# Twelve ring slots, a gather that reads h itself, and expert outputs summed in PSUM

## The chip, the cores and the metric

The kernel runs on one core of a Trainium2 chip. The metric is the device time of one execution in microseconds (us). Everything is float32. One core has a matrix engine (TensorE, PE in the profile; PEld are its loads of the stationary operand), VectorE (DVE), ScalarE (ACT), GpSimd (POOL), and SyncE (SP), which here issues most DMAs. A matmul reads two operands from SBUF, the stationary one (first argument, `[contraction, output rows]`) and the moving one (second argument), and writes one of eight PSUM banks of 128 x 512 float32. A float32 matmul shows as two MATMUL and two LDWEIGHTS records.

## The reference

One encoder block on 256 tokens with 1024 features, then a mixture of experts, then a final norm:

```python
n = rms_norm(h, norm1_g); p = n @ w_in            # q, k, v of two groups of heads
oa = mixer_global(qa, ka, va)                      # 8 heads, all keys, rotary, softmax
ob = mixer_window(qb, kb, vb, sink, rel_bias)      # 8 heads, |i-j| <= 128, bias, sink
h = h + concat[rms_norm(oa, gnorm_a), rms_norm(ob, gnorm_b)] @ w_o
x = rms_norm(h, norm2_g)
gl = x @ w_group + b_group                         # 4 groups, the best one is taken
el = x @ w_expert + b_expert                       # 8 experts a group, the best two are taken
combine[n, e] = softmax weight of the group * normalised weight of the expert
h = h + sum over 32 experts e of
        ((silu(x @ w_gate[e]) * (x @ w_up[e])) * combine[:, e]) @ w_down[e]
out = rms_norm(h, final_g)
```

Each of the 32 experts has three matrices of 1024 x 512 float32, that is 2 MiB each: 96 matrices, 201 MB, all of which are read.

## The kernel before

**Front part.** SP loads the inputs and `w_in`; PE computes q, k, v, the scores, the weighted values and the output projection (`project`) for 8 steps of heads; DVE adds the projections to `h` (128 partitions = tokens, `[t, 1024]` for the two halves t of the tokens). PE begins with three multiplications by a block of zeros (`multiply_zeros`, L1085), which wait for a DVE memset.

**Router.** PE turns `h` (L1093) and multiplies it by the router's weights (`router_logits`, L1249). `ss2`, the sum of squares of each token, comes from ACT (L645, L652); POOL turns it into `rstd2` (L459, L460). DVE computes which two experts each token takes (L879 to L937). Beside it POOL makes `hn = h * norm2_g` (L520), in an order in which each block of 128 features (one `c` of eight, features c, c+8, c+16, ...) lies contiguous, with `norm2_g` broadcast to 128 partitions by a DMA that ACT issues at L642 once the temporary of the attention in the same place (`g2b`) is done with; ACT scales `hn` by `rstd2` (L656).

**Experts.** They are worked on in ten units of 2 or 4 experts (`WAYS = 2,2,4,4,2,2,4,4,4,4`), 128 rows to a unit: 64 or 32 token places for each expert. For unit i:
- DVE makes `pick` (L944), a matrix of zeros and ones: which token goes to which place, and `pick_w` (L952), the same with the expert's weight.
- PE gathers (L1284): `xgT[:, c, :] = hn[:, t, c, :]^T @ pick[:, t, :]`, 8 blocks c times 2 halves t, 32 MATMUL records a unit, into two banks, which ACT (L665) and DVE (L956) copy to `xgT`.
- `products` (L1322, for the first unit `first_gate`, L1383): gate and up, with `xgT` stationary and the weights moving; `silu` (ACT), `product` (DVE); `turn_act` (L1333) transposes the result; `down` and `early_down` (L1339).
- `turn_picks` (L1302) transposes `pick_w`, DVE copies it to `place_w`, and `scatter` (L1373) multiplies it by the unit's output `y_slots`: 4 results of 128 x 512, in two banks used in turn. DVE adds each to `h` (`add_outputs`, L971, 36 additions, and 4 more at the end, L1044), and `sc_free` tells PE that the bank is free.

PE's order in iteration i: first half of the gather of i, `turn_act(i-1)`, second half, `down(i-1)`, gate of i, `scatter(i-2)`, up of i with `turn_picks(i)` in its middle. In `turn_act` the stationary operand is read with a step of four elements:

```python
act_c = act_sb.rearrange("p (k c) -> p c k", c=FC)
last = pe.transpose(ps[TR][:, c * P:(c + 1) * P], act_c[:, c, :], ident)
```

**The ring.** All matrices go through `RING = 11` slots of 16 KB a partition (2 MiB each). The 96 matrices have fixed places in a sequence (`fill_at(unit, gate/up/down, expert)`); number f goes to slot f mod 11, and may be loaded when number f-11 has been used (`wait_used`). The first four experts (units 0 and 1, numbers 0 to 11) are fixed; the other 28 are put in an order that depends on the counts of tokens (`order_ready`, after DVE L1001), and SP reads their numbers with `value_load`. In the front part slots 5 to 10 hold attention data, and SP waits until it is done with before it loads them (L322): number 8 at `projected` 4, number 9 at `weighted_v` 8, number 10 at `projected` 8. Numbers 11 and 12 follow in quarters (L360, L366), as the first gate product uses up slots 0 and 1; the next eleven in halves and quarters (L374); all later ones whole. The last unit's down matrices come in pieces (`LAST_PIECES`).

**The end.** PE multiplies the last pieces (with a multiplication by constants between them, `multiply_constants(1, TR)`, L1268), scatters (L1459), DVE adds to `h`, ACT takes squares (L701), POOL and DVE turn the sums into `rstdf` (L526 to L535, L1075), DVE and ACT scale by `rstdf` and `final_g` (L1078, L706) and the result is stored. `final_g` is broadcast by a DMA at L661.

## Time and profile before

| | |
|---|---|
| median of 3 runs | 571.07 us (570.36 to 571.14) |
| profiled execution | 570.79 us, its span 569.0 us |
| PE, DVE, ACT, POOL busy | 451.1, 116.3, 63.5, 29.1 us |
| mean granted PE clock | 0.902 |
| moved by DMA | 218.72 MB, 384 GB/s over the span |

```profile
span 569.0 us, 6262 instructions
DMA  8989991658999999999999999999999999999992
GB/s 303 382 330 428 424 361 49 285 185 272 384 399 422 429 428 423 428 431 428 423 430 427 427 427 428 428 428 424 430 428 428 426 427 428 428 427 428 418 381 88
PE 49%; DMA 45%; POOL 2%; DVE 1%; issue 1%; SPq 1%; ACT 0%; DVEq 0%; ACTq 0%; POOLq 0%
```

The span is the time from the first to the last instruction; the execution takes 1.8 us more. The second and third line cut the span into 40 slices of 14.2 us: the busy share of the 16 DMA engines in tenths, and what they moved. The last line is the chain of waits that ended last, by engine.

### The profile page before, as it was taken

Reading aid. Unit: us, or ns where it says so; the run is one execution under the profiler, and the core shown is the slowest. Engines: PE = TensorE matmul, PEld = TensorE weight load, DVE = VectorE, ACT = ScalarE, POOL = GpSimd, SP = SyncE. Lnnn points to the kernel's source line nnn. Section 1 sums busy time; section 2 is a strip of 40 time slices with the busy share of each in tenths; the row PEclk is TensorE's granted clock in tenths of the full one; section 3 lists DMA queues with packets and bytes.
Section 4 is the critical chain, followed back from the end, with each engine's and each line's share of the span. In section 5 each row is a group of like instructions: output and inputs, shape, how many; then the busy total and the mean of one; then the engine's idle time right before and its main releaser. Section 6 shows DMA issues by size and latency. Waiting matters only on the chain.

```text
span 569.0 us, 6262 instructions
## 1 busy us (share of the span) xinstructions
PE 451.1 (79%) x2546; PEld 199.9 (35%) x2546; DVE 116.3 (20%) x281; ACT 63.5 (11%) x130; POOL 29.1 (5%) x58
## 2 busy tenths in 40 slices
PE   8999999989999994596999938753855475566874
PEld 3456676564535241141353502230213121311221
DVE  2017764251101210220222202010201002100413
ACT  1125332131000100100101001000000001000103
POOL 0232200220000000000000000000000000000002
PEclk9999999999999996887999978787878767886999
DMA  8989991658999999999999999999999999999992
GB/s 303 382 330 428 424 361 49 285 185 272 384 399 422 429 428 423 428 431 428 423 430 427 427 427 428 428 428 424 430 428 428 426 427 428 428 427 428 418 381 88
DMA packets 27679, 218.72 MB, mean 384 GB/s; under 512 B 5465, under 2 KB 6745, under 8 KB 14849
## 3 DMA queue, kind: packets, MB, share of 16 engines
q1 hardware_dynamic: 23120, 215.09, 91.2%
q10 hardware_dynamic: 4528, 3.22, 1.8%
q8 instruction: 21, 0.34, 0.2%
q14 instruction: 10, 0.07, 0.0%
HBM read 217.23 MB, written 1.06 MB: 384 GB/s over the span
## 4 chain that ended last, share of the span: by engine, by line
PE 49%; DMA 45%; POOL 2%; DVE 1%; issue 1%; SPq 1%; ACT 0%; DVEq 0%; ACTq 0%; POOLq 0%
DMA ring<-in_w_gate_dram 21%; PE bank L1322 19%; DMA ring<-in_w_up_dram 12%; DMA ring<-in_w_down_dram 9%; PE bank L1101 7%; PE bank L1339 6%; PE bank L1284 3%; PE bank L1173 3%; PE bank L1163 2%; DMA g2b<-in_norm_g_dram 2%; PE bank L1373 2%; PE bank L1141 1%; PE bank L1383 1%; PE bank L1152 1%; DMA ring<-in_w_in_dram 1%
## 5 line engine op out<-in xcount | busy, mean ns | idle before, releaser
L1322 PE MATMUL bank<-ring,region_x 128*32 128x512 f32 (+1 forms) x992 | 155.9, 681 | 76.7 <-DMA ring<-in_w_gate_dram 48.8
L1322 PEld LDWEIGHTS bank<-ring,region_x 128*32 128x32 f32 (+1 forms) x992 | 45.0, 129 | 178.8 <-issue 178.8
L1339 PE MATMUL bank<-ring,region_q 128*32 128x512 f32 (+1 forms) x512 | 81.1, 677 | 27.8 <-DMA ring<-in_w_down_dram 25.3
L971 DVE TENSOR_TENSOR h<-h,bank 128x512 f32<-128x512 f32 x36 | 24.7, 687 | 218.0 <-PE bank L1373 218.0
L1339 PEld LDWEIGHTS bank<-ring,region_q 128*32 128x32 f32 (+1 forms) x512 | 23.6, 129 | 77.6 <-issue 72.6
L677 ACT ACTIVATE region_x<-bank 128x512 f32<-128x512 f32 x20 | 11.1, 595 | 286.6 <-PE bank L1373 251.4
L1101 PE MATMUL bank<-ring,region_x 128*128 128x512 f32 x96 | 42.6, 596 | 0.3 <-DMA ring<-in_w_in_dram 0.3
L1284 PEld LDWEIGHTS bank<-region_q,region_t 128*128 128x128 f32 x320 | 37.4, 192 | 8.6 <-issue 8.6
L1284 PE MATMUL bank<-region_q,region_t 128*128 128x128 f32 x320 | 40.1, 278 | 0.3 <-DVE region_q L944 0.3
L1373 PE MATMUL bank<-region_x,region_q 128*128 128x512 f32 x72 | 35.0, 618 | 1.2 <-ACT region_x L677 1.2
L1173 PE MATMUL bank<-ring,region_q 128*128 128x512 f32 x64 | 28.9, 597 | 0.0
L1101 PEld LDWEIGHTS bank<-ring,region_x 128*128 128x128 f32 x96 | 17.8, 190 | 23.2 <-issue 21.6
L526 POOL TENSOR_TENSOR region_t<-h,g2b 128x512 f32<-128x512 f32 x1 | 1.3, 1268 | 442.5 <-ACT region_q L701 442.5
L1373 PEld LDWEIGHTS bank<-region_x,region_q 128*128 128x128 f32 x72 | 11.4, 188 | 24.8 <-DVE h L971 11.8
L665 ACT ACTIVATE region_x<-bank 128x512 f32<-128x512 f32 x10 | 6.0, 597 | 113.8 <-PE bank L1284 113.8
L944 DVE TENSOR_TENSOR region_q<-cst,region_t 128x256 f32<-128x256 f32 x8 | 3.4, 426 | 73.2 <-PE bank L1302 73.2
L1173 PEld LDWEIGHTS bank<-ring,region_q 128*128 128x128 f32 x64 | 11.6, 190 | 12.6 <-issue 12.6
L1163 PE MATMUL bank<-region_v,ring 128*128 128x65 f32 x128 | 15.2, 272 | 0.0
L1163 PEld LDWEIGHTS bank<-region_v,ring 128*128 128x128 f32 x128 | 15.0, 192 | 0.5 <-issue 0.5
L965 DVE TENSOR_TENSOR region_q<-region_q,bank 128x512 f32<-128x512 f32 x10 | 6.9, 688 | 31.1 <-PE bank L1322 31.1
L791 DVE SCALAR_TENSOR_TENSOR h<-bank,stat,h 128x512 f32<-128x512 f32 x8 | 6.0, 751 | 20.6 <-PE bank L1173 17.8
L960 DVE COPY region_q<-bank 128x512 f32<-128x512 f32 x10 | 6.9, 692 | 15.9 <-PE bank L1333 15.9
(192 smaller groups left out, 263.0 us busy)
## 6 DMA issues: line engine op xcount, KB each, us to landing
ring<-in_w_gate_dram SPq DMA_DIRECT2D x28, 2048.0 KB, 32.6
ring<-in_w_up_dram SPq DMA_DIRECT2D x28, 2048.0 KB, 34.0
ring<-in_w_down_dram SPq DMA_DIRECT2D x24, 2048.0 KB, 35.9
ring<-in_w_down_dram SPq DMA_DIRECT2D x10, 1024.0 KB, 13.6
ring<-in_w_up_dram SPq DMA_DIRECT2D x6, 1024.0 KB, 12.2
ring<-in_w_in_dram SPq DMA_DIRECT2D x8, 512.0 KB, 8.5
ring<-in_w_o_dram SPq DMA_DIRECT2D x2, 2048.0 KB, 12.6
ring<-in_w_down_dram SPq DMA_DIRECT2D x8, 512.0 KB, 12.1
```

Source lines behind the costliest of these rows:

```text
L665: act.activation(xgT[:, 0:4, :], ps[GD0][:].rearrange("p (c s) -> p c s", c=4), ACT.Copy).then_inc(xg_act, 1)
L677: act.activation(y_slots[:, 512 * half:512 * half + 512], ps[GD0 + half][:], ACT.Copy).then_inc(y_ready, 1)
L960: dve.tensor_copy(hT, ps[TR][:].rearrange("p (c s) -> p c s", c=FC)).then_inc(hT_ready, 1)
L965: dve.tensor_tensor(act_sb, silu_sb, ps[UP][:], ALU.mult).then_inc(act_done, 1)
L971: dve.tensor_tensor(part, part, ps[SC0 + k % 2][:], ALU.add).then_inc(sc_free, 1)
L1101: return pe.matmul(ps[bank][:], xT[:, c, t * P:(t + 1) * P], cols, start=(c == 0), stop=(c == KC - 1))
L1163: last = pe.matmul(ps[6][:, 65 * l:65 * l + 65], probsT[:, s % 2, kt, l, :], v_sb[:, kt, 2 * g + l // 2, :], start=(kt == 0), stop=(kt == ...
L1173: last = pe.matmul(ps[bank][:], mixT[:, 1 - g, t, c - 4 * g, :], w_o_sb[g][:, c - 4 * g, 512 * half:512 * half + 512], start=(c == 4 * g), ...
L1284: last = pe.matmul(ps[GD0 + b][:, c * P:(c + 1) * P], hn[:, t, 4 * b + c, :], pick[:, t, :], start=(t == 0), stop=(t == TT - 1))
L1322: last = pe.matmul(ps[bank][rows, :], xgT[:, c, rows], slots[fill_slot(f + a)][:, c * F:(c + 1) * F], start=(c == 0), stop=(c == KC - 1))
L1339: last = pe.matmul(ps[GD0 + half][rows, :], hT[:, c, rows], slots[fill_slot(f + a)][:, c * D + 512 * half:c * D + 512 * half + 512], start ...
L1373: last = pe.matmul(ps[SC0 + k % 2][:], place_w[:, (k // 2) * P:(k // 2 + 1) * P], y_slots[:, 512 * (k % 2):512 * (k % 2) + 512], start=Tru ...
```

## The change

- `RING` is 12. The places of `qkT`, `v_sb` and the attention's temporaries, which were tensors of their own (`region_t`, `region_v`, `g2b`), now lie in slot 11 (`late`) and are done with before number 11 is loaded there: SP waits for `sso_ready` 4 (the last sum of squares of the attention's output), between numbers 9 and 10. The refill in pieces now begins with number 12, and both first matrices belong to unit 2, so both need `order_ready`.
- `hn` is gone, with POOL L520, ACT L656 and the broadcast DMA of `norm2_g`. The gather reads `h` itself, as stationary operand with a step of eight elements (`h_cols`). `pick` holds `rstd2` instead of one, and is made by one `tensor_scalar` for each half and expert; so is `pick_w`. `norm2_g` is applied when `xgT` is cut out of PSUM: ACT in four pieces, DVE by a `tensor_tensor`.
- The scatter adds up in four banks (Y0 to Y3) over all units; the 36 additions of DVE and `sc_free` go. `turn_picks` and `turn_act` use the GATE bank: `turn_picks` waits for `silu_done`, `turn_act` for `place_ready`. `place_w` has two buffers.
- At the end DVE adds `h` and the four banks into `h_sum`. `final_g` is spread by matmuls (`spread_final_g`) in place of the multiplications by constants, and copied by ACT; the sum for `rstdf` is one instruction of DVE, only the power is left to POOL.
- At the start PE multiplies 4.5 blocks of zeros from a constant and waits for nothing, where it had multiplied 3 after a memset.

```diff
-RING = 11
+RING = 12
+        late = slots[QKT_SLOT]
+        q_tmp = late[:, 3080:3592].rearrange("p (h d) -> p h d", h=8)
-        hn = region_t[:, 0:2048].rearrange("p (t c k) -> p t c k", t=TT, c=KC)
+        h_cols = h.rearrange("p t (k c) -> p t c k", c=KC)
+        h_sum = slots[TAIL_SLOT][:, 2048:4096].rearrange("p (t d) -> p t d", t=TT)
...
             load(1, 1, 1, 3)
+            sp.wait_ge(sso_ready, 4)
+            load(1, 2, 1, 3)
             sp.wait_ge(projected, 8)
             load(1, 2, 0, 2)
...
+            sp.wait_ge(order_ready, 1)
+            experts = order_of(2, range(1))
+            for c in range(PIECES):
+                if c < PIECES - 1:
+                    sp.wait_ge(gate_pieces, c + 1)
+                else:
+                    sp.wait_ge(gate_done, 1)
+                load_piece(2, 0, 0, c, PIECES)
+                if c == 0:
+                    experts += order_of(2, range(1, 2))
+                if c == 2:
+                    experts += order_of(2, range(2, 4))
+                load_piece(2, 0, 1, c, PIECES)
...
-                pool.tensor_tensor(hn[:, t].rearrange("p c k -> p k c"), h[:, t, :].rearrange("p (k c) -> p k c", c=KC),
-                                   g2b[:].rearrange("p (k c) -> p k c", c=KC), ALU.mult).then_inc(hg_ready, 1)
...
-                act.activation(hn[:, t], hn[:, t], ACT.Copy, scale=rstd2[:, t:t + 1]).then_inc(hn_ready, 1)
...
-                act.activation(xgT[:, 0:4, :], ps[GD0][:].rearrange("p (c s) -> p c s", c=4), ACT.Copy).then_inc(xg_act, 1)
+                for c in range(4):
+                    last = act.activation(xgT[:, c, :], ps[GD0][:, c * P:(c + 1) * P], ACT.Copy, scale=g2_rows[:, c:c + 1])
...
+                for t in range(TT):
+                    for a in range(n_e):
+                        last = dve.tensor_scalar(pick[:, t, rows * a:rows * (a + 1)], iota1[:, 0:rows],
+                                                 ranks[:, t, e0 + a:e0 + a + 1], rstd2[:, t:t + 1], ALU.is_equal, ALU.mult)
...
-                    dve.tensor_tensor(part, part, ps[SC0 + k % 2][:], ALU.add).then_inc(sc_free, 1)
...
-                        last = pe.matmul(ps[GD0 + b][:, c * P:(c + 1) * P], hn[:, t, 4 * b + c, :], pick[:, t, :],
+                        last = pe.matmul(ps[GD0 + b][:, c * P:(c + 1) * P], h_cols[:, t, 4 * b + c, :], pick[:, t, :],
...
-                    pe.wait_ge(place_ready, i)
+                    pe.wait_ge(silu_done, i + 1)
...
-                    pe.wait_ge(sc_free, 4 * i + k + 1)
-                    last = pe.matmul(ps[SC0 + k % 2][:], place_w[:, (k // 2) * P:(k // 2 + 1) * P],
-                                     y_slots[:, 512 * (k % 2):512 * (k % 2) + 512], start=True, stop=True)
+                    last = pe.matmul(ps[Y0 + k][:], place_w[i % 2][:, (k // 2) * P:(k // 2 + 1) * P],
+                                     y_slots[:, 512 * (k % 2):512 * (k % 2) + 512], start=(i == 0), stop=False)
...
-            pe.wait_ge(zeros_ready, 1)
-            multiply_zeros(3)
+            zeros = nc.const_aps.tensor(0.0, (P, 512), F32)
+            for cols in (512, 512, 512, 512, 256):
+                pe.matmul(ps[6][:, 0:cols], zeros[:, 0:P], zeros[:, 0:cols], start=True, stop=True)
...
+            def spread_final_g(half, bank):
+                for k in range(4):
+                    c = 4 * half + k
+                    last = pe.matmul(ps[bank][:, k * P:(k + 1) * P], final_g_cols[:, c:c + 1].broadcast_to([P, P]), ident,
+                                     start=True, stop=True)
+                last.then_inc(final_g_turned, 1)
...
             last_products(0)
+            spread_final_g(0, UP)
             last_products(1)
-            multiply_constants(1, TR)
+            spread_final_g(1, GATE)
             last_products(2)
-            multiply_constants(1, TR)
             last_scatter(0)
             last_products(3)
...
+            dve.wait_ge(ssf_ready, 3)
+            dve.scalar_tensor_tensor(rstdf[:, 0:1], ssf[:, 0:1], EPS, ssf[:, 1:2], ALU.add, ALU.add).then_inc(mean_ready, 1)
```

## Rows read from the trace of the kernel before

**Rows 1.** The span cut into stages: busy time of each engine, PEclk, DMA share, GB/s.

```profile
85.00:95.00 10.00, 10.00 (x53) 6.79 (x53) 4.89 (x13) 3.27 (x8) 0.73 (x2) 1.00 0.01 2
95.00:128.00 33.00, 31.51 (x159) 19.99 (x159) 12.75 (x53) 7.70 (x14) 6.91 (x8) 1.00 0.59 223
128.00:141.00 13.00, 12.87 (x72) 5.75 (x70) 2.81 (x10) 2.47 (x3) 0.00 (x0) 1.00 0.81 258
141.00:153.00 12.00, 11.12 (x70) 6.45 (x66) 2.40 (x4) 0.60 (x1) 0.00 (x0) 1.00 1.02 409
...
210.00:550.00 340.00, 236.49 (x1442) 86.63 (x1434) 43.68 (x72) 14.61 (x27) 0.00 (x0) 0.84 1.01 427
```

**Rows 2.** DMA issues of the page: KB each, median us from issue to landing.

```profile
ring<-in_w_gate_dram SPq DMA_DIRECT2D x28, 2048.0 KB, 32.6
```

**Rows 3.** SP's DMA issues around the router, from the timeline: start, us.

```profile
96.23 2.06 SPq L322 DMA_DIRECT2D ring<-in_w_up_dram  x2
113.07 0.33 SPq L322 DMA_DIRECT2D ring<-in_w_down_dram  x1
128.58 0.33 SPq L360 DMA_DIRECT2D ring<-in_w_down_dram  x1
```

**Rows 4.** The chain of waits from 97 to 127 us: start, us, what.

```profile
99.47 11.92 DMA g2b<-in_norm_g_dram
...
117.42 0.56 POOL stat L460
...
118.00 0.43 DVE region_q L879 x2
...
123.61 2.92 PE bank L1284 x24
```

**Rows 5.** Timeline of the router: the last sum of squares, the last logits.

```profile
114.95 0.20 ACT L652 ACTIVATION_READ_ACCUMULATOR region_q<-h 128x1 f32 x1
...
115.49 2.03 PE L1249 MATMUL bank<-region_t,region_x 128*128 128x36 f32 x16
```

**Rows 6.** PE records by source line: ns min/median/max, first and last start, form.

```profile
L1383 PEld LDWEIGHTS bank<-ring,region_x x32: 132/137/137, 126.6 to 134.8; 128*64 128x64 f32 x32
L1302 PEld LDWEIGHTS bank<-cst,region_q x20: 138/140/143, 131.1 to 540.5; 128*128 128x128 f32 x20
L1333 PEld LDWEIGHTS bank<-cst,region_q x40: 195/209/218, 145.7 to 545.6; 128*128 128x128 f32 x40
L1333 PE MATMUL bank<-cst,region_q x40: 277/283/385, 145.8 to 545.8; 128*128 128x128 f32 x40
L1284 PEld LDWEIGHTS bank<-region_q,region_t x320: 186/192/201, 123.6 to 490.7; 128*128 128x128 f32 x160
```

**Rows 7.** Timeline of PE: runs of matmuls with few moving columns.

```profile
96.04 1.89 PE L1163 MATMUL bank<-region_v,ring 128*128 128x65 f32 x16
...
145.84 0.64 PE L1333 MATMUL bank<-cst,region_q 128*128 128x128 f32 x4
```

**Rows 8.** DVE and ACT operations by source line: ns min/median/max.

```profile
L944 DVE TENSOR_TENSOR region_q<-cst,rank x2: 416/420/425, 123.0 to 132.0; 128x256 f32<-128x256 f32 x2
L725 DVE TENSOR_SCALAR region_x<-region_x,gT x8: 346/350/354, 5.7 to 11.9; 128x256 f32<-128x256 f32 x8
L665 ACT ACTIVATE region_x<-bank x10: 597/597/598, 125.7 to 488.9; 128x512 f32<-128x512 f32 x10
```

**Rows 9.** Timeline of PE's start.

```profile
1.58 5.26 PE L1085 MATMUL bank<-region_t 128*128 128x512 f32 x6 [1.58 <-DVE region_t L720]
...
7.12 5.39 PE L1101 MATMUL bank<-ring,region_x 128*128 128x512 f32 x12 [0.28 <-DMA ring<-in_w_in_dram]
```

**Rows 10.** Timeline of the end: last square, last power, last two outputs.

```profile
562.64 0.19 ACT L701 ACTIVATION_READ_ACCUMULATOR region_q<-h 128x1 f32 x1
...
563.64 0.54 POOL L535 TENSOR_TENSOR stat<-stat 128x1 f32<-128x1 f32 x1
563.71 1.41 DVE L1078 SCALAR_TENSOR_TENSOR region_t<-h,stat,g2b 128x512 f32<-128x512 f32 x2 [0.31 <-POOL stat L533]
```

More of the change, by code:

```diff
@@ L675, in down_out @@
                 for half in range(2):
+                    if i == UNITS - 1:
+                        act.wait_ge(final_g_turned, half + 1)
+                        act.activation(final_gb[:, 512 * half:512 * half + 512], ps[(UP, GATE)[half]][:], ACT.Copy).then_inc(final_g_cut, 1)
                     act.wait_ge(down_done, 2 * i + 1 + half)
@@ L965, in product @@
                 dve.tensor_tensor(act_sb, silu_sb, ps[UP][:], ALU.mult).then_inc(act_done, 1)
-            def add_outputs(i):
-                for k in range(4):
-                    dve.wait_ge(scattered, 4 * i + k + 5)
-                    part = h[:, k // 2, 512 * (k % 2):512 * (k % 2) + 512]
-                    dve.tensor_tensor(part, part, ps[SC0 + k % 2][:], ALU.add).then_inc(sc_free, 1)
             def places_out(i):
                 dve.wait_ge(picks_turned, i + 1)
-                dve.wait_ge(scattered, 4 * i + 4)
-                dve.tensor_copy(place_w, ps[PW][:, 0:256]).then_inc(place_ready, 1)
+                if i > 1:
+                    dve.wait_ge(scattered, 4 * i)
+                dve.tensor_copy(place_w[i % 2], ps[PICKS0 if i == 0 else GATE][:, 0:256]).then_inc(place_ready, 1)
             make_picks(rank1, 0, 2)
-            dve.engine_nop().then_inc(sc_free, 2)
             k_w = mark(dve.tensor_tensor(w2, w1, e2, ALU.mult))
@@ L1042, in _ @@
                 dve.wait_ge(scattered, 4 * UNITS + k + 1)
-                part = h[:, t, 512 * half:512 * half + 512]
-                dve.tensor_tensor(part, part, ps[(SC0, SC1, GATE, UP)[k]][:], ALU.add).then_inc(sc_free, 1)
+                dve.tensor_tensor(h_sum[:, t, 512 * half:512 * half + 512], h[:, t, 512 * half:512 * half + 512],
+                                  ps[Y0 + 2 * t + half][:], ALU.add).then_inc(summed, 1)
             over = dve.value_load(over_flag[0:1, 0:1], min_val=0, max_val=1)
@@ L1048, in _ @@
                 ov_nT_sb = slots[3].rearrange("p (c t) -> p c t", c=16)
+                link(dve.tensor_tensor(weight_over, weight_over, bcast(rstd2, 2, EXPERTS), ALU.mult))
                 for t in range(TT):
@@ L1064, in _ @@
                         for half in range(2):
-                            part = h[:, t, 512 * half:512 * half + 512]
+                            part = h_sum[:, t, 512 * half:512 * half + 512]
                             last = dve.tensor_tensor(part, part, ps[3 + half][:], ALU.add)
@@ L1082, in _ @@
         def _(pe):
-            def multiply_zeros(n):
-                for _ in range(n):
-                    pe.matmul(ps[6][:], zeros[:, 0:P], zeros[:, P:P + 512], start=True, stop=True)
-            pe.wait_ge(zeros_ready, 1)
-            multiply_zeros(3)
+            zeros = nc.const_aps.tensor(0.0, (P, 512), F32)
+            for cols in (512, 512, 512, 512, 256):
+                pe.matmul(ps[6][:, 0:cols], zeros[:, 0:P], zeros[:, 0:cols], start=True, stop=True)
             def turn(dst, srcs, done):
@@ L1331, in turn_act @@
                 pe.wait_ge(act_done, i + 1)
+                pe.wait_ge(place_ready, i + 1)
                 for c in range(FC):
-                    last = pe.transpose(ps[TR][:, c * P:(c + 1) * P], act_c[:, c, :], ident)
+                    last = pe.transpose(ps[GATE][:, c * P:(c + 1) * P], act_c[:, c, :], ident)
                 last.then_inc(act_turned, 1)
@@ L1398, in _ @@
             for k in range(2 * TT):
-                last = pe.transpose(ps[SC0][0:EXPERTS, k * P:(k + 1) * P], (rank1, weight)[k // TT][:, k % TT, :], ident)
+                last = pe.transpose(ps[RANKS][0:EXPERTS, k * P:(k + 1) * P], (rank1, weight)[k // TT][:, k % TT, :], ident)
             last.then_inc(ranks_turned, 1)
@@ L1481, in _ @@
                     else:
-                        pe.wait_ge(sc_free, 4 * UNITS + 2)
+                        pe.wait_ge(summed, 4)
                     for b in range(2):
                         for c in range(4):
-                            last = pe.transpose(ps[5 + b][:, c * P:(c + 1) * P], hn[:, t, 4 * b + c, :], ident)
+                            last = pe.transpose(ps[5 + b][:, c * P:(c + 1) * P], h_cols[:, t, 4 * b + c, :], ident)
                     last.then_inc(ov_turned, 1)
```

244 lines of the change are left out of this document (105 added, 139 removed).

## The prediction, made before the changed kernel ran

> **What bounds the kernel now.** I read the page's busy shares first, then the span cut into stages. From 210 to 550 us the DMA engines are busy all the time (share 1.01) and move 427 GB/s, while PE works 236 of 340 us [rows 1]. There only bytes count. Before that lies the hole that the change can reach: from 85 to 95 us 2 GB/s are moved, from 95 to 128 us 223 GB/s, from 128 to 141 us 258 GB/s [rows 1]. The reason is in SP's issues: nothing is loaded after the transfer issued at 113.07 us until a slot comes free at 128.58 us [rows 3], though 96 - 11 = 85 matrices are still to come. So the time is: the moment T0 at which slot 0 begins to come free, plus the matrices still missing then, plus what idles until the queue is full, plus an end after the last piece.
>
> T0 hangs on a chain: ACT issues the broadcast of `norm2_g` at 99.47 us, it lands 11.92 us later, then POOL makes `hn` and the power (the last ends at 117.98), DVE decides (118.00 on), PE gathers from 123.61 on [rows 4].
>
> **The change part by part.**
>
> *The twelfth slot.* One matrix is 2048 KB = 2.097 MB [rows 2]; at 427 GB/s [rows 1] that is 4.91 us. It counts in full if number 11 is there before T0 and the DMA engines are the bound afterwards. SP issues two matrices from 96.23 us [rows 3]; number 11 comes right behind them, since `sso_ready` 4 falls in the 0.2 us before 99.47 [rows 4], where ACT issued the next thing in its program. Three matrices from 96.2 on take 14.7 us, to 111; number 10, issued at 113.07, takes 4.9, to 118. T0 is ten us later. Its wait has number 10 queued behind it on SP, which waits for something later anyway. After T0 the same bytes come free at the same pace, so the lead of one matrix stays. **-4.9 us.** Its other end is 0, if the lead is lost somewhere. The pieces of refill are as many and as large as before; both now wait for `order_ready`, which comes with DVE L1001, behind the gather's end at 126.53 [rows 4] and some two us before 128.58; the first `value_load` falls into that time. 0.
>
> *The router's chain.* Without broadcast, POOL L520 and ACT L656, `rstd2` needs only the last sum of squares, there at 114.95 + 0.20 = 115.15 [rows 5], and POOL's two small operations (0.56 for the power [rows 4], less for the other): 116.1. Now the logits are late: PE ends them at 115.49 + 2.03 = 117.52 [rows 5]. DVE starts at 117.55 instead of 118.00 [rows 4]: **-0.45** (bounds -0.9 and 0).
>
> *The first picks* are on the chain. One `tensor_tensor` of 256 columns takes 0.42 us; now four `tensor_scalar` of 64. The nearest row is `tensor_scalar` on 256 columns, 0.35 [rows 8]. Four as one, 0.35, is the lower end (-0.07); four at 0.2 one after the other, 0.8, the upper (+0.4). They don't depend on each other and overlap in part: **+0.15**. The eight and eight of a four-way unit lie on DVE beside the second half of the up product, and after 210 us beside 104 us in which PE waits anyhow [rows 1]; uncovered before 210 they might cost 2 us once.
>
> *The gather reads with a step of eight.* This is the unknown. LDWEIGHTS takes 137 ns for 64 columns (L1383) and 192 for 128 (L1284) [rows 6]: 0.86 ns a column and 82 fixed. A transpose with packed columns takes 140 (L1302), 0.45 a column; the same with a step of four elements, 16 bytes, 209 (L1333) [rows 6]: (209 - 82)/128 = 0.99 ns a column. So a step costs a transpose's load 69 ns. What decides is how far apart the pairs come: n of them last n - 1 spacings and one record of 0.28 [rows 6]. Where only 65 columns move, the load sets it: 16 in 1.89 us is 0.107 [rows 7], near 128 x 0.86. The gather's 24 in 2.92 us [rows 4] make 0.115; the four stepped transposes in 0.64 [rows 7] make 0.119. No row has a stepped load that is no transpose. Three answers:
>  (a) the load goes at the slower of its own pace and the stepped one, 0.99 ns a column: spacing 0.127, +0.012 a record;
>  (b) the 69 ns come on top of 0.107: 0.176, +0.061;
>  (c) a plain float32 load needs two stepped passes of 0.127: 0.254, +0.139.
> Of these I take (a): 0.86 and 0.99 lie side by side, and it looks as if the plain load already runs slowly enough to hide most of the step.
> What one record costs the end: 24 lie before T0, 8 before the third quarter of slots 0 and 1 is free, so 32 in full. The 32 of unit 1 lie between the freeing of the up slots and of the down slots. There the queue has just run out: 13 us at 258 and 12 us at 409 GB/s are 8.26 MB moved from 128 to 153 us [rows 1], of the 8.39 MB of the four slots freed; I count 1 us of slack (0 to 2). After that slots come free faster than they are filled, and more delay is hidden. Cost: 32x + max(0, 32x - 1). (a) **+0.4**, (b) 1.95 + 0.95 = 2.9, (c) 4.45 + 3.45 = 7.9 us.
>
> The Trainium skill bears on this: "SBUF — State Buffer", section "Door 1: The DMA port swizzle", says that SBUF is read in lines of 16 bytes and that each step to a new line pays a penalty, so that a step of four float32 is the last free one. By that rule the gather, at 32 bytes, is slowed, as in (b) or (c), and the change loses half its gain or all of it. The trace agrees in so far as L1333 pays 69 ns, and that already at four elements. The same skill, "TensorE: Matmul & The Clock Gate", section "LDWEIGHTS", puts a load at the columns divided by 1.2 in ns; the 0.86 ns a column of the plain load fits that, the 0.45 of a transpose does not.
>
> *xgT* is cut in four pieces by ACT. Whole it took 0.60 us [rows 8]. The first piece can take no longer, and PE has 8 gather records, 0.92 us, in between; the next chunks are further apart. 0. In later units it lies beside the second half of the gather. If it didn't: four times 0.6 less 0.6, 1.8 us, and only before 153 us.
>
> *Scatter, 36 additions gone, new waits.* DVE's 36 additions stood beside PE. `turn_picks` waits for `silu_done`, and silu (one ACT pass) has the scatter and half the up product to be done in; behind it on PE stand the rest of the up product and so the next slots. `turn_act` waits for `place_ready`, which DVE gives before the product that `turn_act` waits for anyway. 0; the bound is one ACT pass, 0.6 [rows 8], in unit 1, which has no scatter ahead. Scatters without `sc_free` can only gain, and PE has time there.
>
> *The start.* Before, six zero records take 5.26 us from 1.58 on, 0.86 each, and the first real ones follow at 7.12, 12 in 5.39 us or 0.43 each [rows 9]: the first go at half the rate, which is that of the lower level of PE's clock (1.2 of 2.4 GHz), though the granted clock is given as 1.00. Nine records of 512 columns now start some 0.65 us earlier, at about 0.95. If they stay slow as long as before, until between 6 and 7.1 us less those 0.65, some three are left to run at 0.43: end between 7.1 and 7.6. If the rate changes at the same moment as before, up to 7.9. If it came at once, they would end long before 7.12, and the data would be late next. From there to the router PE works without a gap, so a late start reaches T0. **+0.25** (0 to +0.75).
>
> *The end.* The last square is there at 562.83, POOL's last power starts only at 563.64, and DVE's two outputs run from 563.71 to 565.12 [rows 10]. Now the sum is one DVE operation (0.2) behind the square, the power (0.54) follows: 562.9 + 0.2 + 0.1 + 0.54 = 563.8 for the second half, whose output of 0.7 ends at 564.5; the first half's is done by then. **-0.6** (-1.0 to 0). `spread_final_g` stands where constants were multiplied.
>
> Sum: -4.9 - 0.45 + 0.15 + 0.4 + 0.25 - 0.6 = **-5.15 us**. The profiled execution took 570.79 (span 569.0 and 1.8 around it): 565.6; the median of the runs is 0.28 higher: **565.9 us**.
>
> **The rivals.**
> 1. *The stepped load costs its 69 ns in full (b).* -5.55 + 2.9 = -2.65: 568.4. For it: L1333; against it: the two paces side by side.
> 2. *Slower: the stepped load needs two slow passes (c).* Place: the gathers of units 0 and 1. -5.55 + 7.9 = +2.35: 573.4. It decides from 64x - 1 = 5.55, a spacing of 0.115 + 0.102 = 0.217 us or more. For it: a plain load costs twice a transpose's packed one a column (0.86 to 0.45), as if it read everything twice.
> 3. *The lead is lost* (number 11 is late or PE is the bound between 153 and 210 us): only the small terms are left, about 570.8. Against it: share 1.01 for 340 us.
> 4. *More is won*: PE, without waits for banks, frees slots sooner between 128 and 160 us, where the queue runs dry: another 2 us, 563.9.
>
> **How the numbers follow.** Forecast 0.54, rival 1 0.20, rival 2 0.11, rival 3 0.07, rival 4 0.08. The forecast's own range is 564.8 to 567.2, from its small terms. To leave out no more than two in ten the range takes in rivals 1 and 4 and ends short of rivals 2 and 3: **563.6 to 570.0**. A change under 0.2% (1.1 us) can't be told from none. Faster: forecast, rivals 1 and 4, less a little for unseen stalls, 0.80; within 0.2%: most of rival 3, 0.08; slower: rival 2 and such stalls, 0.12.
>
> **What would show it.** Number 11 issued near 99.7 us; DMA idle from 118 to about 128; the chain runs through PE's logits, not through a broadcast; L1284's successor at 24 in about 3.2 us and LDWEIGHTS near 209 ns (261 for rival 1, 335 for rival 2); first refill near 128.9; 427 GB/s from 210 us on and the last piece about 4.6 us sooner; the last output ending 1.7 us behind the last square instead of 2.3. It would be wrong if the first refill came later than 130 us or the DMA share fell below 1 after 160 us.

## The result and the profile after

The changed kernel takes **578.88 us** (median of 4 runs, 576.27 to 579.52), the kernel before 571.11 in the same session: ratio 1.0117, 95% interval 1.0085 to 1.0149. It is 7.8 us slower. The profiled execution took 579.32 us, its span is 577.1. So 2.2 us lie outside the span, where the kernel before has 1.8.

The page of the kernel after, its span, DMA share and GB/s (40 slices), and the weight loads of the gather:

```profile
span 577.1 us, 6390 instructions
...
DMA  8979992925979999999999999999999999999981
GB/s 307 379 297 433 420 363 104 363 116 185 372 265 427 405 404 429 433 422 430 425 428 429 426 426 428 426 430 425 430 428 424 432 424 429 430 425 428 421 343 75
...
L1263 PEld LDWEIGHTS bank<-region_q,h 128*128 128x128 f32 x320 | 77.7, 334 | 9.1 <-issue 8.2
```

The same windows as in [rows 1] (length, then busy us and instructions of PE, PEld, DVE, ACT and POOL, granted clock, DMA share, GB/s), kernel after:

```profile
95.00:128.00 33.00, 32.26 (x134) 20.72 (x133) 13.38 (x56) 5.01 (x11) 2.19 (x6) 0.88 0.65 255
128.00:141.00 13.00, 12.87 (x62) 8.08 (x63) 3.27 (x13) 3.01 (x6) 0.00 (x0) 0.92 0.42 141
141.00:153.00 12.00, 12.00 (x59) 6.39 (x55) 2.06 (x8) 0.60 (x1) 0.00 (x0) 1.00 0.90 319
153.00:160.00 7.00, 6.12 (x29) 5.56 (x30) 1.38 (x2) 1.14 (x4) 0.00 (x0) 1.00 0.92 383
160.00:190.00 30.00, 29.12 (x134) 16.03 (x132) 5.74 (x20) 2.93 (x7) 0.00 (x0) 1.00 0.92 357
190.00:210.00 20.00, 20.00 (x132) 6.68 (x132) 0.00 (x0) 1.58 (x3) 0.00 (x0) 1.00 0.99 395
210.00:550.00 340.00, 258.99 (x1508) 120.00 (x1504) 37.68 (x125) 19.01 (x49) 0.00 (x0) 0.89 1.01 427
```

The plateau from 210 us on is what it was, 427 GB/s. More is moved ahead of T0: 255 against 223 GB/s from 95 to 128 us. The 32 GB/s more are 1.06 MB; the kernel before also moved its two broadcasts there, so the twelfth matrix (2.10 MB) is the gain. (Without its early load, but otherwise with the changed front part, it is 191 GB/s, in e9 and e5 below.) But the hole behind it is deeper, 141 against 258 GB/s and 319 against 409 [rows 1], and it lasts: the full rate holds only from 210 us on.

One instruction has become slower, the weight load of the gather (count, then minimum, median and maximum in ns, start of the first and last):

```profile
L1263 PEld LDWEIGHTS bank<-region_q,h x320: 312/335/340, 125.6 to 501.5; 128*128 128x128 f32 x160
```

Before, it took 192 ns [rows 6]. From the chain of waits of the kernel after (start, duration, engine, what, line, records):

```profile
117.67 5.89 PE bank L1247 x8
...
124.52 0.99 DVE region_q L934 x4
...
125.56 6.00 PE bank L1263 x24
...
150.08 4.00 PE bank L1263 x16
...
180.56 4.00 PE bank L1263 x16
...
214.94 4.00 PE bank L1263 x16
...
237.81 39.02 DMA ring<-in_w_gate_dram
```

The first 24 records take 6.00 us where they took 2.92 [rows 4]: their spacing is (6.00 - 0.28)/23 = 0.249 us. It is the same in the 16 of unit 1, (4.00 - 0.28)/15 = 0.248, at a granted clock of 1.00, so the lower clock in part of the first gather (0.92 from 128 to 141 us) is not the reason. And the chain stays on PE, through the gathers of units 1, 2 and 3, until it goes over to a DMA at 237.81.

SP's issues of the kernel after; the second row is the first refill, which was at 128.58 [rows 3]:

```profile
99.06 13.94 SPq L324 DMA_DIRECT2D ring<-in_w_down_dram  x2
...
133.77 17.91 SPq L361 DMA_DIRECT2D ring<-in_w_gate_dram  x12
```

The prediction had named two signs that it would be wrong: a first refill later than 130 us, and a DMA share below 1 after 160 us. Both are there, 133.77 and 0.92.

### The profile page after: what moved, and what is told of

It is laid out like the page before. It is cut to its first block, busy times and chain, and to the rows that moved or that the text cites. A ratio compares the mean times of both kernels' runs of the same rounds, so it can differ in the third digit from the quotient of the medians.

```text
span 577.1 us, 6390 instructions
## 1 busy us (share of the span) xinstructions
PE 482.0 (84%) x2562; PEld 244.6 (42%) x2562; DVE 110.0 (19%) x353; ACT 67.9 (12%) x160; POOL 23.6 (4%) x53
## 3 DMA queue, kind: packets, MB, share of 16 engines
HBM read 216.19 MB, written 1.06 MB: 376 GB/s over the span
## 4 chain that ended last, share of the span: by engine, by line
PE 55%; DMA 41%; DVE 1%; SPq 1%; issue 1%; DVEq 0%; POOL 0%; ACT 0%
DMA ring<-in_w_up_dram 33%; PE bank L1301 18%; PE bank L1080 7%; PE bank L1263 7%; DMA ring<-in_w_gate_dram 7%; PE bank L1319 6%; PE bank L1152 5%; PE bank L1142 2%; PE bank L1120 1%; PE bank L1352 1%; PE bank L1365 1%; PE bank L1072 1%; PE bank L1131 1%; PE bank L1247 1%; DMA ring<-in_w_in_dram 1%; SPq L324 1%
## 5 line engine op out<-in xcount | busy, mean ns | idle before, releaser
L1263 PEld LDWEIGHTS bank<-region_q,h 128*128 128x128 f32 x320 | 77.7, 334 | 9.1 <-issue 8.2
L1263 PE MATMUL bank<-region_q,h 128*128 128x128 f32 x320 | 80.5, 407 | 0.7 <-DVE region_q L934 0.7
L1319 PE MATMUL bank<-ring,region_q 128*32 128x512 f32 (+1 forms) x512 | 73.1, 609 | 9.3 <-DMA ring<-in_w_down_dram 6.7
L667 ACT ACTIVATE region_x<-bank 128x512 f32<-128x512 f32 x20 | 11.1, 595 | 237.8 <-PE bank L1352 222.3
L648 ACT ACTIVATE region_x<-bank,gT 128x128 f32<-128x128 f32 x40 | 11.4, 367 | 139.9 <-PE bank L1263 139.9
L520 POOL TENSOR_TENSOR ring<-ring 128x512 f32<-128x512 f32 x1 | 1.3, 1275 | 452.8 <-ACT region_q L691 452.8
L1142 PEld LDWEIGHTS bank<-ring 128*128 128x128 f32 x128 | 15.0, 192 | 0.5 <-issue 0.5
L1142 PE MATMUL bank<-ring 128*128 128x65 f32 x128 | 15.2, 272 | 0.0
L950 DVE TENSOR_TENSOR region_x<-bank,gT 128x512 f32<-128x512 f32 x10 | 6.9, 692 | 33.5 <-PE bank L1263 33.5
L943 DVE TENSOR_SCALAR region_q<-cst,sorted_rw 128x32 f32<-128x32 f32 (+1 forms) x56 | 12.4, 301 | 0.0
L934 DVE TENSOR_SCALAR region_q<-cst,sorted_rw,stat 128x32 f32<-128x32 f32 (+1 forms) x56 | 12.4, 299 | 0.0
```

The source lines that it names most:

```text
L648: last = act.activation(xgT[:, c, :], ps[GD0][:, c * P:(c + 1) * P], ACT.Copy, scale=g2_rows[:, c:c + 1])
L667: act.activation(y_slots[:, 512 * half:512 * half + 512], ps[GD0 + half][:], ACT.Copy).then_inc(y_ready, 1)
L934: last = dve.tensor_scalar(pick[:, t, rows * a:rows * (a + 1)], iota1[:, 0:rows], ranks[:, t, e0 + a:e0 + a + 1], rstd2[:, t:t + 1], ALU.i ...
L943: last = dve.tensor_scalar(pick_w[:, t, rows * a:rows * (a + 1)], iota1[:, 0:rows], ranks[:, t, e0 + a:e0 + a + 1], weights[:, t, e0 + a:e ...
L950: dve.tensor_tensor(xgT[:, 4:8, :], ps[GD1][:].rearrange("p (c s) -> p c s", c=4), bcast(g2_rows[:, 4:8], 2, P), ALU.mult).then_inc(xg_dve, 1)
L1142: last = pe.matmul(ps[6][:, 65 * l:65 * l + 65], probsT[:, s % 2, kt, l, :], v_sb[:, kt, 2 * g + l // 2, :], start=(kt == 0), stop=(kt == ...
```

## The experiments

Fifteen experiments ran, one of them (e12) the changed kernel again. Times are medians; a ratio is to the kernel before in the same session (571.14 to 571.63 us), with its 95% interval.

### The step by itself, taken away and put in

**e2_after_packed**, the kernel after, with the gather reading 128 columns that lie together. This leaves out the order of the features, so the experts compute something else, with the same work; the same holds for e3, e5, e8 to e11 and e15:

```diff
-last = pe.matmul(..., h_cols[:, t, 4 * b + c, :], pick[:, t, :],
+last = pe.matmul(..., h[:, t, (4 * b + c) * P:(4 * b + c + 1) * P], pick[:, t, :],
```

> The changed kernel, but the gather reads h in packed blocks of 128 columns. This leaves out the order of the features (the experts get wrong rows of the weights), the work is the same. Theory 1: 8.0 us (between 7.6 and 8.6) less than the changed kernel, that is 570.3 to 571.3 us, first refill issued near 129.5 us instead of 133.8. Theory 2: no more than 3 us less, over 575.9 us.

Measured: 567.49 us, 0.9929 (0.9905 to 0.9952). That is lower than either expectation had it. The step alone costs 578.88 - 567.49 = **11.4 us** by the medians and 10.7 by the two ratios, with some 2 us of uncertainty either way. Windows and chain of e2:

```profile
128.00:141.00 13.00, 12.87 (x72) 5.75 (x72) 4.35 (x18) 2.66 (x4) 0.00 (x0) 1.00 0.67 219
141.00:153.00 12.00, 11.12 (x70) 6.45 (x68) 2.07 (x3) 1.14 (x4) 0.00 (x0) 1.00 0.99 383
153.00:160.00 7.00, 7.00 (x35) 2.77 (x33) 0.00 (x0) 1.19 (x2) 0.00 (x0) 1.00 1.00 360
160.00:190.00 30.00, 29.12 (x180) 12.81 (x180) 5.74 (x20) 1.74 (x5) 0.00 (x0) 1.00 1.02 422
190.00:210.00 20.00, 20.00 (x158) 8.97 (x154) 5.74 (x20) 2.71 (x7) 0.00 (x0) 1.00 1.02 429
```

```profile
117.52 0.43 DVE region_q L868 x2
...
123.60 4.31 PE bank L1263 x24
...
203.66 33.91 DMA ring<-in_w_up_dram
```

Against the rows of after, the five windows from 128 to 210 us lack (219 - 141) x 13 + (383 - 319) x 12 + (360 - 383) x 7 + (422 - 357) x 30 + (429 - 395) x 20 kB = 4.25 MB; at 427 GB/s that is 10.0 us, of the 11.0 between the two profiled executions (579.32 and 568.30). More than half of it, 2.63 MB, is missing after 160 us, where I had counted on cover. Here the chain leaves PE at 203 us, not at 237.

**e1_before_stepped**, the kernel before with `hn` laid out in `h`'s order, so that its gather steps by eight. POOL's multiplication and ACT's scaling then go through `hn` in the other order, but take what they took (2.35 and 1.14 us, before 2.37 and 1.15):

```diff
-hn = region_t[:, 0:2048].rearrange("p (t c k) -> p t c k", t=TT, c=KC)
+hn = region_t[:, 0:2048].rearrange("p (t k c) -> p t c k", t=TT, c=KC)
...
-act.activation(hn[:, t], hn[:, t], ...)
+act.activation(hn[:, t].rearrange("p c k -> p k c"), hn[:, t].rearrange("p c k -> p k c"), ...)
```

> The kernel before, with one edit: hn is stored in the order of h, so that the gather reads it with a step of eight elements, as the changed kernel does. Theory 1 (a plain float32 load makes two slow passes when its columns are stepped): records 0.249 us apart instead of 0.115, 24 x 0.134 = 3.2 us before the first gate product, 8 x 0.134 = 1.1 before the third quarter of slots is free, 32 x 0.134 - 1 = 3.3 in unit 1: 7.6 us slower, 578.7 us, LDWEIGHTS 335 ns. Theory 2 (the stepped load is mostly hidden by the DMA queue, and the loss comes from the clock drop at 116 us, the picks and the end): at most 2 us slower, under 573.1 us.

Measured: 580.89 us, 1.0158 (1.012 to 1.0195), +9.6 us. The weight load of e1:

```profile
L1284 PEld LDWEIGHTS bank<-region_q,region_t x320: 312/335/338, 123.7 to 504.2; 128*128 128x128 f32 x160
```

So the cost belongs to the stepped operand, not to the ring, the PSUM banks or the new picks. It is the price that rival 2 put on it; that the load really makes two passes, no run shows.

### How large a step

**e8_steps_by_unit** gives each of the ten units a step of its own; one execution.

```diff
+steps_of = (8, 8, 1, 2, 4, 8, 1, 2, 4, 8)
+def block_of(t, c):
+    s = steps_of[unit_now[0]]
+    return h[:, t].rearrange("p (b k s) -> p b s k", k=P, s=s)[:, c // s, c % s, :]
```

> The changed kernel with another step in each unit's gather: 8, 8, 1, 2, 4, 8, 1, 2, 4, 8 elements (features come in the wrong order where it isn't 8). Theory X (SBUF is read in lines of 16 bytes, each new line costs): packed 192 ns for a LDWEIGHTS, step 2 in between or as packed, steps 4 and 8 alike, 335 ns. Theory Y (the cost grows with the step): step 4 clearly below step 8, near 260 ns, as the transposes with step 4 (209 ns, 69 more than packed) would say if the 69 ns were simply added.

Its weight loads in the gathers of units 1, 2, 3 and 8, steps 8, 1, 2 and 4 in this order:

```profile
L1270 PEld LDWEIGHTS bank<-region_q,h x32: 312/335/336, 147.9 to 155.7; 128*128 128x128 f32 x32
...
L1270 PEld LDWEIGHTS bank<-region_q,h x32: 186/192/202, 178.4 to 182.3; 128*128 128x128 f32 x32
...
L1270 PEld LDWEIGHTS bank<-region_q,h x32: 192/196/208, 208.8 to 212.9; 128*128 128x128 f32 x32
...
L1270 PEld LDWEIGHTS bank<-region_q,h x32: 308/329/329, 430.5 to 438.2; 128*128 128x128 f32 x32
```

Steps of 1, 2, 4 and 8 take 192, 196, 329 and 335 ns: a cliff between 8 and 16 bytes, and nearly flat on both sides of it. The execution took 573.47 us, near the kernel in which units 0 and 1 step and the others are packed (574.42, next).

### Where the step costs time

The same edit in some units only, on the base of e2: in units 0 and 1 (**e10_stepped_early**), in 2 to 9 (**e11_stepped_late**), in 0 to 2 (**e15_stepped_012**); and the kernel after once more beside the first two (**e12_after_again**).

```diff
-if unit_now[0] < 2:      # e10; e11 swaps the two results
+if unit_now[0] < 3:      # e15
     return h_cols[:, t, c, :]
 return h[:, t, c * P:(c + 1) * P]
```

> The changed kernel, with the step of eight only in the gathers of units 0 and 1, and packed blocks (wrong order of features) in units 2 to 9. By the place named in the prediction (only units 0 and 1 reach the end) the whole loss stays: 578.9 us. If unit 2, which also comes before the queue is full for good, matters as well: 1 to 3 us less, 576 to 578 us.

> The reverse: packed in units 0 and 1, the step of eight in units 2 to 9, which costs PE 4 us a unit. By the prediction the DMA queue hides all of it: 567.5 us, as the packed kernel. If not, up to 3 us more, and the DMA share falls below 1 somewhere after 180 us.

> The changed kernel once more, beside the others on the same chip: 578.9 us. Its trace tells whether the fall of the granted clock stands at 116 to 123 us again. If it is a property of the kernel's program it comes at the same place; if it wanders, it comes elsewhere between 112 and 130 us, and the mean over runs holds a part of it.

> The step of eight in units 0, 1 and 2, packed blocks (wrong order of features) in units 3 to 9. Stepped in units 0 and 1 only it was 574.4 us, in all units 578.8. If unit 2 is the rest: 577 to 578.8 us. If it is not (the rest is the clock's fall, which hits only some programs): 574.4 to 575.5 us.

| stepped in | us | ratio (95%) |
|---|---|---|
| none (e2) | 567.49 | 0.9929 (0.9905 to 0.9952) |
| units 2 to 9 (e11) | 568.87 | 0.9953 (0.9932 to 0.9974) |
| units 0 and 1 (e10) | 574.42 | 1.0063 (1.0033 to 1.0093) |
| units 0 to 2 (e15) | 578.13 | 1.0126 (1.0108 to 1.0144) |
| all (e12) | 578.75 | 1.0115 (1.0095 to 1.0136) |

By the medians units 0 and 1 cost 6.9 us and unit 2 another 3.7; both are clear of the intervals, which leave each some 2 us of room. The 0.6 of units 3 to 9 and the 1.4 of units 2 to 9 alone (e11) are inside them. The two parts alone, 6.9 and 1.4, fall short of the 11.4 of all: by the medians, a late gather hurts when the queue is behind already. I had expected 576 to 578.9 for e10. The windows of e10, then those of e15:

```profile
160.00:190.00 30.00, 29.13 (x152) 13.55 (x150) 5.74 (x20) 2.93 (x7) 0.00 (x0) 1.00 0.99 386
190.00:210.00 20.00, 20.00 (x152) 6.68 (x149) 4.36 (x18) 1.58 (x3) 0.00 (x0) 1.00 1.02 427
```

```profile
160.00:190.00 30.00, 29.13 (x134) 16.03 (x132) 5.74 (x20) 2.93 (x7) 0.00 (x0) 1.00 0.97 379
190.00:210.00 20.00, 20.00 (x136) 6.44 (x136) 0.36 (x2) 1.57 (x3) 0.00 (x0) 1.00 1.00 400
```

In e10 the rate is back at 427 from 190 us on; with unit 2 stepped too it is at 400 until 210. From 128 to 210 us e15 moves 0.75 MB less than e10, or 1.8 us; the two profiled executions lie 2.8 us apart (576.62 and 573.79). e10 and e12 ran in one session, e2 and e15 in others, so differences across them carry the sessions' own, up to half a microsecond.

### The slot, its lead, and its capacity

**e9_packed_eleven_used** is e2 with the loads in the order and at the distance of the kernel before: twelve slots are there, eleven fills are ahead. **e5_packed_no_lead** is e2 with number 11 issued behind the first refill's wait instead of early.

```diff
 load(1, 1, 1, 3)                 # both
-sp.wait_ge(sso_ready, 4)
-load(1, 2, 1, 3)
...
+if c == 0:                       # e5; e9: waits on FILLED_BY[f - 11]
+    load(1, 2, 1, 3)
```

> The packed kernel with twelve slots, but SP's program and PE's waits for pieces of the kernel before: number f is loaded when number f - 11 has been used, so that only eleven slots are ever full. Theory of capacity (until 153 to 160 us the queue runs dry, so that then all free slots are filled, and what counts is how many slots there are, not when the twelfth was filled): 4.9 us more than the packed kernel, 572.4 us. Rival (the twelfth slot gave nothing, as holding back its first load cost only 0.7 us; what the packed kernel gained came from the router and the missing broadcasts): 567.5 to 568.5 us.

> The packed kernel of the second experiment (the gather takes packed blocks, so features come in the wrong order), with the load of number 11 held back until the first quarter of slot 0 comes free: twelve slots, but only eleven filled when the refill begins. If the twelfth slot is worth its lead (one matrix at 427 GB/s), this is 4.9 us slower than the packed kernel: 572.4 us. If the lead is lost later anyway, no change: 567.5 us.

e9: 572.24 us, 1.0009 (0.9996 to 1.0023), so the slot is worth 572.24 - 567.49 = **4.75 us**, or 4.4 if each is taken against the kernel before in its own session (+0.6 and -3.8). e5: 568.2 us, 0.9934 (0.9914 to 0.9954), only 0.7 us above e2, inside the intervals. The windows of e5:

```profile
128.00:141.00 13.00, 12.87 (x76) 6.36 (x76) 4.98 (x23) 3.61 (x7) 0.00 (x0) 1.00 0.68 242
141.00:153.00 12.00, 11.12 (x69) 6.30 (x67) 2.17 (x4) 1.14 (x4) 0.00 (x0) 1.00 1.03 423
153.00:160.00 7.00, 7.00 (x36) 2.88 (x34) 0.00 (x0) 1.19 (x2) 0.00 (x0) 1.00 1.00 412
```

The queue of e2 runs dry from 128 to 160 us (219, 383, 360 GB/s) and e5 moves more in those gaps (242, 423, 412). That is 1.14 MB, a good half of the late matrix. The reading that fits both runs is that what counts is how many slots are there for the queue until PE is ahead of it, not how early the twelfth is filled.

### The small terms

**e3_packed_tt_picks**: e2 with the picks in one `tensor_tensor`, `rstd2` left out. **e4_after_short_start**: the kernel after with three zero blocks in place of five. **e14_after_one_constant**: the kernel after with a fourth of the constants' products ahead of the ranks.

```diff
-for a in range(n_e):                          # e3, for each t
-    last = dve.tensor_scalar(pick[...], iota1[:, 0:rows], ranks[...], rstd2[:, t:t + 1], ALU.is_equal, ALU.mult)
+dve.tensor_tensor(to, bcast(...iota1[:, 0:rows]...), bcast(ranks[...], 3, rows), ALU.is_equal)
-for cols in (512, 512, 512, 512, 256):        # e4
+for cols in (512, 512, 512):
-multiply_constants(4, GATE)                   # e14
+multiply_constants(1, GATE)
```

> As the packed kernel, and the picks and weighted picks made by one tensor_tensor each as in the kernel before; rstd2 is left out of the picks, so the experts get rows that are not normalised. If the four tensor_scalar cost what the trace of the changed kernel shows (0.99 us against 0.44 on the chain), this is 0.55 us faster than the packed kernel. If their waits in later units also cost something, 1 us or more.

> The changed kernel with 3 blocks of zeros at the start instead of 4.5. Theory A (the granted clock falls at 116 us because of where the start puts PE's work): the granted clock stays 1.00 from 116 to 123 us and the time falls by about 1.6 us, to 577.3 us, less what a slower first chunk costs (up to 0.7 us). Theory B (the fall comes from the router stretch itself): granted clock 0.5 from about 117 to 123 us as before, 578.9 us or up to 0.7 us more.

> The changed kernel with one multiplication by constants ahead of the choice instead of four. If the block of constants at half clock (5.9 us instead of 3.1) is what makes the choice late, this is 1.5 to 2 us faster than the changed kernel, 577 us, with the gather beginning near 123.5 us. If the clock then falls during the gather or the first gate product instead, part of it is lost again: 577.5 to 579 us.

e3: 567.18 us, 0.9901 (0.9862 to 0.9939), inside e2's interval: 0.3 us, not told apart. e4: 578.8, 1.0109 (1.0075 to 1.0144), no difference. e14: 577.6, 1.0107 (1.0091 to 1.0122); 1.3 us less than after by the medians, but the intervals overlap, so inconclusive. What e4 and e14 asked of the clock is answered at the end of this document.

### Versions that keep the slot and pack the columns

**e6_sorted_in_place** sorts `h` in place by ACT between the router's transposes and the gather, through a spare region, and lets the last additions on DVE read `h` in the sorted order, where neighbouring features lie 128 elements apart. **e7_sorted_tt_picks** also lets that pass multiply by `rstd2`, takes the picks in one `tensor_tensor` and divides the root out in the last addition. **e13_sorted_early** is e7 with the first half of `h` sorted some 10 us earlier. All three compute the whole reference.

```diff
+act.activation(h_spare, h[:, t].rearrange("p (k c) -> p c k", c=KC), ACT.Copy)
+act.wait_ge(rstd2_ready, t + 1)                       # e7, e13
+act.activation(h[:, t].rearrange("p (c k) -> p c k", c=KC), h_spare, ACT.Copy, scale=rstd2[:, t:t + 1])   # e6: no scale
```

> The changed kernel, complete, but ACT puts h in the order of the gather, in place, through a spare 1024 columns, between its last square (114.6 us) and its exponentials; the gather then reads packed columns, and DVE reads h with a step in its four last additions. Four passes of 1.15 us end near 119.3 us, before the picks at 122.6: nothing on the chain, so the time of the packed kernel, 567.5 us. If stepped reads slow ACT or DVE as they slow the weight load (twice as long), ACT ends near 122 us and the last addition costs 0.7 us more: 568.5 to 569 us.

> As the one before, and rstd2 is put into h by the same ACT pass (and taken out again in DVE's last additions), so that the picks are one tensor_tensor each, as in the kernel before. 0.55 us less on the chain than the sorted kernel: 566.9 us.

> The complete kernel of experiment 7 (h sorted in place by ACT with rstd2 in it, picks by one tensor_tensor), but the first half of h is sorted at once when it has been turned (110 us), and only the second after the last square. In experiment 6 a stepped ACT pass took 2.06 us instead of 1.1 and the four passes ended at 122.4 us, 1.1 us too late for the picks. With two of them out of the way the picks start at about 122.6 us and the first refill comes at about 128.6 us instead of 129.4: 567.5 us. Without an effect: 568.4 us.

e6: 568.57 us, 0.9951 (0.993 to 0.9972). e7: 568.42, 0.994 (0.9916 to 0.9964). e13: **568.08, 0.9939 (0.9925 to 0.9952)**, 3.2 us faster than before and 10.8 faster than the change; among themselves the three are not told apart, so the gains expected of e7 and e13 over e6 don't show. Groups of e6 by line:

```profile
L646 ACT ACTIVATE region_q<-h x2: 2059/2060/2061, 116.1 to 119.2; 128x1024 f32<-128x1024 f32 x2
...
L648 ACT ACTIVATE h<-region_q x2: 1057/1057/1057, 118.2 to 121.3; 128x1024 f32<-128x1024 f32 x2
...
L1034 DVE TENSOR_TENSOR ring<-h,bank x4: 1032/1054/1092, 554.0 to 558.0; 128x512 f32<-128x512 f32 x4
```

Paid once, the stepped read costs ACT 1.0 us per 1024 columns, beside the router's work; paid in the gather it is 320 slow loads on PE.

## Why the prediction was wrong

The range ended at 570.0; the time is 578.88. The sign was missed too. Two steps of the working failed: the pace of the stepped weight load, and the cover that I counted on behind unit 1.

**The gather's step: the step that failed.** I chose answer (a), a spacing of 0.127 us and +0.4 us. Measured are 0.249 us and 335 ns, within 2% of answer (c) (0.254, 335), to which I gave 0.11. What misled me was the nearest row: a transpose with a step of four pays 69 ns [rows 6], and I took its pace, 0.99 ns a column, for the pace of any stepped load. But the plain load's own pace, 0.86, hides nothing of the step; it pays 335 - 192 = 143 ns, twice what the transpose pays. Both rows lay beside each other, and the doubling between packed loads (0.86 against 0.45), which I quoted for rival 2, was the better guide. The Trainium skill, "SBUF — State Buffer", section "Door 1: The DMA port swizzle", spoke against (a), and the trace agrees with its direction. It gives four float32 as the last free step, and that does not hold here: four pay nearly the full price (329 ns, e8). It also says that a line of 16 bytes has to be hit at least twice for the full rate, and with that e8 agrees: two float32 are free (196).

**"After that more delay is hidden": failed as well.** Rival 2's own price, 7.9 us for units 0 and 1, was near what they cost, 6.9. Its total of 573.4 falls short by 5.5 because unit 2 costs 3.7 us, where I had put the cover from unit 2 on, and because of the small terms. I had taken 1 us of slack from the bytes of before, whose queue was on time; with the queue some 7 us behind, PE stays the bound through unit 3, as the chain up to 237.81 shows. (Rival 3 had named PE as the bound from 153 to 210 us, as a way to lose the lead; it had no price for it beyond that.) Of the 5.5, 3.5 are the later units less what the 7.9 had too much (11.4 - 7.9), 1.8 are the small terms below, and 0.2 the sessions.

**The slot: right in size, wrong in reason.** Forecast 4.9, measured 4.4 to 4.75. But I had it as the lead of a matrix loaded before T0, and e5 shows that the early load is worth only 0.7 of it.

**The router's chain: right.** DVE starts at 117.52 in e2 against 118.00 [rows 4]: -0.48 for -0.45.

**The picks: mis-sized.** Four `tensor_scalar` take 0.99 us on the chain, against 0.42 for the one before: +0.57, over my upper end of +0.4. (e3, which takes them back, is only 0.3 us faster, so how much of this reaches the end is not shown.) Source rows of the kernel after:

```profile
L934 DVE TENSOR_SCALAR region_q<-cst,rank,stat x8: 306/310/315, 124.5 to 138.7; 128x64 f32<-128x64 f32 x8
```

Each is 0.31 long, hardly less than 256 columns take (0.35, [rows 8]), and they follow each other by 0.23: a fourth of the columns is not a fourth of the time, and the overlap is small.

**The start: not settled.** Timeline of the kernel after, the zero records and the first real ones:

```profile
0.77 5.58 PE L1067 MATMUL bank<-const-float32-0.0 128*128 128x512 f32 x10 [0.77 <-PEq L1509]
...
6.73 3.67 PE L1080 MATMUL bank<-ring,region_x 128*128 128x512 f32 x8 [0.38 <-DMA ring<-in_w_in_dram]
```

In this trace the zero records end before the first data are there, and what PE waits for is the DMA; the first real one comes 0.4 us earlier than before, not 0.25 later. But the same zero records last 5.5 to 7.05 us in the traces of the experiments. From the chain of e9:

```profile
0.77 7.05 PE bank L1071 x10
7.82 5.15 PE bank L1084 x12
```

There PE waits for no data, and neither does it in e6 to e8, e10, e11, e14 and e15. The first real product starts between 6.73 and 7.66 us over all traces with these records, on both sides of the 7.12 before. So the late change of rate that I forecast is real, and its cost lies between -0.4 and +0.5 us, differing from trace to trace. e4, without two of the blocks, shows no difference in time.

**The end: nothing gained.** Timeline of the kernel after:

```profile
570.57 0.16 DVE L1054 SCALAR_TENSOR_TENSOR stat<-stat 128x1 f32<-128x1 f32 x1 [0.52 <-issue]
570.62 0.19 ACT L691 ACTIVATION_READ_ACCUMULATOR region_q<-ring 128x1 f32 x1
...
570.81 1.43 POOL L523 TENSOR_TENSOR stat<-stat 128x1 f32<-128x1 f32 x2 [1.10 <-DVE stat L1054]
571.77 1.42 DVE L1060 SCALAR_TENSOR_TENSOR ring<-ring,stat 128x512 f32<-128x512 f32 x2 [0.36 <-POOL stat L523]
```

I had the first half's power done early. But the sum for it comes at 570.57 only, behind DVE's last addition and 0.52 us of issue, so both powers queue on POOL: 1.43 us. From the last square (570.81) to the end of the outputs (573.19) it is 2.38 us, against 565.12 - 562.83 = 2.29 before [rows 10]: +0.1 for my -0.6.

**The sum.** Without the step I forecast -5.55; e2 gives 567.49 - 571.27 = -3.8. The terms that the traces put off by a plain amount are the picks, +0.4, the end, +0.7, the slot, +0.15 to +0.5, and one that I had overlooked: I took the 1.8 us outside the span as fixed, and with the changed kernel and all that are built on it they are 2.2 to 2.4, +0.45 (no run tells why). Together that is 1.7 to 2.05, which covers the 1.8. Two more vary from trace to trace and can't be split off: the start, and a gather of 4.31 us in e2's chain where 2.92 was expected, from a half-rate stretch that I had not foreseen (below). Whether the latter reaches the end is not shown: in e3 the gather takes 2.94 us and the first refill comes at 128.78 instead of 130.11, yet its median is only 0.3 lower. With the step: 11.4 for 0.4.

## What to carry to other kernels

Before a copy is dropped and its reader made to step through memory, look for the reader's own kind of row, and count how often it reads: a stepped operand that is read by 320 weight loads costs more than one stepped pass of another engine that packs it. Where no row shows the operation, don't take the pace of a different form as a ceiling; give the doubling a real chance. And slack that was measured on a kernel in time holds only as long as the kernel stays in time: price a delay again with the queue as late as the delay makes it.

## What the runs showed of the hardware

**Steps.** A float32 weight load of 128 columns takes 192, 196, 329 and 335 ns at steps of 1, 2, 4 and 8 elements. ACT's copy of 128x1024 takes 1.06 us packed and 2.06 us with a step of eight on its input (e6). DVE's addition of 128x512, one operand in PSUM, takes 1.05 us when it reads `h` 128 elements apart, the other two in order (e6), and 0.69 with all three in order (after).

**The clock.** TensorE's granted clock drops to its lower level (1.2 of 2.4 GHz) in stretches of 3 to 7 us near the router. From 116 to 123 us, the kernel after and the kernel before:

```profile
116.00:123.00 7.00, 7.00 (x17) 4.10 (x17) 4.16 (x27) 0.42 (x2) 0.00 (x0) 0.53 0.48 204
...
126.00:130.00 4.00, 4.00 (x18) 4.00 (x18) 2.11 (x13) 0.20 (x1) 0.00 (x0) 0.58 0.00 0
```

```profile
116.00:123.00 7.00, 5.78 (x31) 3.87 (x30) 4.77 (x29) 1.65 (x4) 1.79 (x3) 1.00 0.73 291
```

The first two rows are of after, the third of before. The first fall makes the products of constants (L1247) take 5.89 us in the chain, so that the matmuls that rank the choices start at 123.40 us; before, they started at 121.82. None of my terms held that. Whether these 1.6 us reach the end is not shown: in e4 the fall is shorter (117.4 to 120.8), in e14 it comes from 122.2 to 129 and the ranks start at 121.61, and in both the first refill comes 1.4 or 1.5 us sooner than 133.77; but the medians are only 0.1 and 1.3 us lower, within the intervals. Theory A of e4 does not hold as it stands: without two of the zero blocks the fall is still there.

It falls from 116.4 to 123.2 us in after and from 116.5 to 123.3 in e12. In the other traces it falls elsewhere: in e3 from 116.8 to 120.3, in e5 from 117.0 to 123.7, in e2 from 123.1 to 126.5 and in e13 from 123.2 to 126.6, inside the gather (hence gathers of 4.31 and 4.54 us); in e8 and e10 from 124.5 to 128, in e15 from 125.4 to 128.7, in e1 from 125.9 to 129.2; in before, e6, e7, e9 and e11 nowhere there.

A packed gather of 24 records takes 2.92 to 2.94 us at the full clock (before, e3, e9, e11) and 4.31 in e2. A stepped one takes 6.00 us in after, with the clock down for more than half of it, and 5.98 in e4, at a granted clock of 1.00. Its loads take 312 to 340 ns at either clock, and the fall costs the stepped gather nothing.

What makes the clock fall stays open. PE was busy without a gap from 116 to 123 us in after and had gaps in before, but that is in part the fall's own work, since the constants last longer; and e2 and e10, busy without a gap from 116 to 120 us as well, kept the full clock there. One hint is that the fall goes with the start: where the ten zero records last 6.9 us or more (e6, e7, e9, e11) there is no fall, where they last 6.2 to 6.8 us (e8, e10, e14, e15) it comes at 122.2 us or later, and where they last 5.5 to 5.9 us (after, e12, e2, e3, e5, e13) it comes between 116.4 and 123.2 us. That is one trace of each kernel, no experiment. Until it is settled, differences of one or two microseconds between two such kernels may hold some of it.
